# Stick-breaking attention of a two-block network in three units of key blocks, the first of them ahead of the last value slab

## What is computed

```
z = q @ k^T * 64**-0.5                            # per head, 512 x 512
log_beta = log_sigmoid(z)
log_1m = where(strict, log_sigmoid(-z), 0)        # strict: key position < query position
tail = reverse_cumsum(log_1m) - log_1m            # over the keys
a = where(strict, exp(log_beta + tail), 0)
o = a @ v;   out = concat(o over heads) @ w_out   # added to the residual
```

## Time and profile before

| what | value |
|---|---|
| time, median of 3 runs | 2701.61 us (2700.36 to 2703.32) |
| the profiled execution, its own time | 2699.93 us |
| its span in the profile | 2697.7 us |
| PE, DVE, ACT busy over the span | 97%, 58%, 34% |
| last matmul of the value slabs | 1989.12 us |
| first score of pairs 1, 4 and 5 | 2009.36, 2049.38, 2062.72 us |
| first matmul of the projection | 2106.82 us |

### The profile page before, as it was taken

One profiled execution on the slowest core, in us unless ns is written; L12 is line 12 of the kernel. 1 busy time (PEld: TensorE's weight loads), 2 busy tenths in 40 slices (PEclk: granted clock), 3 DMA queues, 4 the chain that ended last, 5 costly groups with the idle time before them and its releaser, 6 DMA issues.

```text
span 2697.7 us, 32184 instructions
## 1 busy us (share of the span) xinstructions
PE 2616.2 (97%) x12690; PEld 2142.3 (79%) x12690; DVE 1568.2 (58%) x1934; ACT 908.8 (34%) x1186; POOL 0.2 (0%) x4
## 2 busy tenths in 40 slices
PE   8999999989999999999999999999999999999999
PEld 6888887778888877877788888888876788888887
DVE  6444456676444457476564766566356566574745
ACT  4222243443222234433442423234136343432322
POOL 0000000000000000000000000000000000000000
PEclk9999999999999999999999999999999999999999
DMA  5222232003222223211331222323210132122222
GB/s 175 94 94 93 94 120 79 32 32 112 100 94 93 94 94 103 87 63 63 109 110 63 95 97 91 109 81 126 94 63 1 54 134 94 64 94 94 97 102 81
DMA packets 36595, 240.67 MB, mean 89 GB/s; under 512 B 3952, under 2 KB 6912, under 8 KB 8320
## 3 DMA queue, kind: packets, MB, share of 16 engines
q1 hardware_dynamic: 35008, 234.12, 25.3%
q10 hardware_dynamic: 1472, 4.94, 0.5%
HBM read 236.94 MB, written 2.10 MB: 89 GB/s over the span
## 4 chain that ended last, share of the span: by engine, by line
PE 89%; DVE 7%; ACT 2%; issue 1%; DMA 0%; SPq 0%; DVEq 0%; ACTq 0%
PE ps L469 24%; PE ps L471 23%; PE ps L470 23%; PE ps L1028 1%; PE ps L981 1%; PE ps L953 1%; PE ps L487 1%; PE ps L486 1%; PE ps L485 1%; PE ps L497 1%; PE ps L1013 1%; PE ps L581 1%; PE ps L583 1%; PE ps L582 1%; DVE w_lo L1663 1%
## 5 line engine op out<-in xcount | busy, mean ns | idle before, releaser
L469 PE MATMUL ps<-op_hi,w_hi 128*128 128x512 f32 x2160 | 854.0, 395 | 21.1 <-DVE op_lo L1577 15.2
L470 PE MATMUL ps<-op_lo,w_hi 128*128 128x512 f32 x2160 | 844.0, 391 | 0.0
L471 PE MATMUL ps<-op_hi,w_lo 128*128 128x512 f32 x2160 | 843.8, 391 | 0.0
L1082 ACT ACTIVATE w_hi<-w_raw 128x2048 fp32r<-128x2048 f32 x217 | 414.2, 1909 | 527.5 <-PE ps L471 394.7
L1663 DVE TENSOR_TENSOR w_lo<-w_raw,w_hi 128x2048 fp32r<-128x2048 f32 x217 | 497.0, 2292 | 32.5 <-ACT w_hi L1082 17.2
L469 PEld LDWEIGHTS ps<-op_hi,w_hi 128*128 128x128 f32 x2160 | 407.7, 189 | 113.2 <-issue 20.3
L470 PEld LDWEIGHTS ps<-op_lo,w_hi 128*128 128x128 f32 x2160 | 407.6, 189 | 89.1 <-issue 4.9
L471 PEld LDWEIGHTS ps<-op_hi,w_lo 128*128 128x128 f32 x2160 | 407.4, 189 | 85.8
L1628 DVE SCALAR_TENSOR_TENSOR x<-ps,x 128x512 f32<-128x512 f32 x134 | 92.6, 691 | 347.3 <-PE ps L471 339.5
L469 PE MATMUL ps<-h_hi,w_hi 128*128 128x512 f32 x692 | 273.4, 395 | 0.0
L471 PE MATMUL ps<-h_hi,w_lo 128*128 128x512 f32 x692 | 273.4, 395 | 0.0
(11 more groups left out here) (285 smaller groups left out, 2951.3 us busy)
## 6 DMA issues: line engine op xcount, KB each, us to landing
w_raw<-in_wstream_dram SPq DMA_DIRECT2D x217, 1024.0 KB, 4.9
w_raw<-in_wstream_dram SPq DMA_DIRECT2D x8, 256.0 KB, 7.2
x<-in_x_dram SPq DMA_DIRECT2D x4, 512.0 KB, 6.8
cr_m<-in_mem_dram ACTq DMA_DIRECT2D x2, 1024.0 KB, 4.7
out_dram<-x SPq DMA_DIRECT2D x3, 512.0 KB, 2.6
ev_s<-in_alibi_dram ACTq DMA_DIRECT2D x1, 1024.0 KB, 4.8
m_c<-in_rope_dram ACTq DMA_DIRECT2D x1, 704.0 KB, 4.0
pl_p<-in_p_dram ACTq DMA_DIRECT2D x1, 512.0 KB, 3.5
```

The costliest lines, as they stand in the source:

```text
L469: mm_(o, w_hi[:, c % 4, w], hi[:, k, 0:cols], start=(k == 0), stop=False)
L470: mm_(o, w_hi[:, c % 4, w], lo[:, k, 0:cols], start=False, stop=False)
L471: mm = mm_(o, w_lo[:, c % 4, w], hi[:, k, 0:cols], start=False, stop=(k == kt - 1))
L1082: f_(w_hi[:, c % 4, :], w_raw[:, c % 2, :], ACT.Copy).then_inc(w_hi_ready, 1)
```

## The change

Blocks 3 and 2 become one unit of 384 columns in one pair of banks; block 1 and block 0 are units of their own, with 384 and 512 columns (`UNITS`). Each unit keeps its banks: unit 0 has 4 and 5, unit 1 has 6 and 7, unit 2 has 2 and 3 (the ones of the value slab before the last). The out results take banks 0 and 1 by turns. Unit u of pair t waits for the weights of unit u of pair t - 1. ACT and DVE handle a unit with one instruction where they had two for blocks 3 and 2.

The softplus of unit 0 has places of its own for even t (`od_s_even`, `od_hi_even`, `od_lo_even`), over buffers that are free then and not over `op_hi`. The scores of units 0 and 1 of pair 0 stand ahead of the last value slab on PE, and unit 0's softplus on ACT and DVE runs beside that slab; DVE also makes `w_lo` of the second slab of three still ahead before it. The mask matrix is rounded earlier. PE's order per pair becomes

```diff
-TRI = 13 * P
-TRI_A = 11 * P
+TRI = 10 * P
+FAR = 3 * P
+UNITS = [(3, 2), (1,), (0,)]
+UNIT_COLUMNS = [FAR, 3 * P, 4 * P]
+UNIT_AT = [0, FAR, FAR + 3 * P]
...
-Z_BANKS = [4, 6, 0]
...
-def cut_at(t, kb):
-
-    return [9 * P, 6 * P, 2 * P * (1 + t % 2), P * (t % 2)][kb]
...
-def weight_at(t, kb):
-
-    return [7 * P, 4 * P, 2 * P, P * (t % 2)][kb]
+def block_at(kb):
+
+    return [2, 1, 0, 0][kb], P if kb == 2 else 0
...
+        with ExitStack() as s:
+            od_s_even = sb("od_s_even", [P, 2, FAR], FP32, s)
+        with ExitStack() as s:
+            od_lo_even = sb("od_lo_even", [P, 2, FAR], FP32R, s)
...
+        with ExitStack() as s:
+            od_hi_even = sb("od_hi_even", [P, 2, FAR], FP32R, s)
...
+        def unit_bank(u):
+
+            return [4, 6, pair_of(AT_ODD + ODD_SLABS - 2)][u]
+
+        def unit_z(u):
+
+            return ps[:, unit_bank(u):unit_bank(u) + 2, 0:UNIT_COLUMNS[u]]
+
+        def stick_bank(t):
+
+            return pair_of(AT_ODD + ODD_SLABS - 1) + t % 2
+
+        def unit_parts(t, u):
+
+            at, w = UNIT_AT[u], UNIT_COLUMNS[u]
+            if u == 0 and t % 2 == 0:
+                tiles = (od_s_even, od_hi_even, od_lo_even)
+            else:
+                tiles = (od_s, od_hi, od_lo)
+            return [tile[:, :, at:at + w] for tile in tiles]
...
-            for d in range(8, 12):
+            for d in range(8, 11):
                 to_positions(AT_ODD + d)
-            pe.wait_ge(acc_free, AT_ODD + ODD_SLABS + 2)
...
-                return Z_BANKS[(NB * t + NB - 1 - kb) % len(Z_BANKS)]
...
+            def stick_scores(t, u):
+                if t:
+                    pe.wait_ge(a_made, 3 * (t - 1) + u + 1)
+                for kb in UNITS[u]:
+                    b, at = unit_bank(u), block_at(kb)[1]
+                    for j in range(2):
+                        mm_(ps[:, b + j, at:at + SEQ - kb * P], od_k[64 * j:64 * j + 64, t, kb * P:(kb + 1) * P],
+                            od_q[64 * j:64 * j + 64, t, kb * P:SEQ], start=(kb == UNITS[u][0]), stop=False,
+                            skip_group_check=True)
...
+                mm.then_inc(z_done, 1)
...
+            def stick_exponent(t, u):
+
+                pe.wait_ge(softplus_cut, 3 * t + u + 1)
...
+                    for kb in UNITS[u]:
+                        z = block_at(kb)[1]
+                        for b in range(kb, NB):
+                            (of, at), w = block_at(b), SEQ - b * P
+                            a0 = z + (b - kb) * P
+                            _, hi, lo = unit_parts(t, of)
+                            for part in (hi, lo):
+                                mm = mm_(ps[:, unit_bank(u) + j, a0:a0 + w], od_later[:, 0 if b == kb else 1, :],
                 mm.then_inc(arg_ready, 1)
...
-                pe.wait_ge(a_made, NB * (t + 1))
+                pe.wait_ge(a_made, 3 * t + 3)
-                for kb in range(NB):
-                    at, w = weight_at(t, kb), SEQ - kb * P
+                for kb in reversed(range(NB)):
+                    (of, at), w = block_at(kb), SEQ - kb * P
+                    at += UNIT_AT[of]
                     for j in range(2):
-                        mm = mm_(ps[64 * j:64 * j + 64, 2 + t % 2, kb * P:SEQ],
+                        mm = mm_(ps[64 * j:64 * j + 64, stick_bank(t), kb * P:SEQ],
...
             pe.wait_ge(later_ready, 1)
-            for kb in (3, 2):
-                stick_scores(0, kb)
+            stick_scores(0, 0)
+            stick_scores(0, 1)
+            to_positions(AT_ODD + ODD_SLABS - 1)
+            n["op"] += KT
+            pe.wait_ge(acc_free, AT_ODD + ODD_SLABS + 1)
             for t in range(PAIRS):
-                stick_exponent(t, 3)
-                stick_scores(t, 1)
-                stick_scores(t, 0)
+                if t:
+                    stick_scores(t, 1)
+                stick_scores(t, 2)
+                if t == 1:
+                    pe.wait_ge(acc_free, AT_ODD + ODD_SLABS + 2)
                 if t:
                     stick_out(t - 1)
+                stick_exponent(t, 0)
+                if t < PAIRS - 1:
+                    stick_scores(t + 1, 0)
+                stick_exponent(t, 1)
                 stick_exponent(t, 2)
-                stick_exponent(t, 1)
-                if t < PAIRS - 1:
-                    stick_scores(t + 1, 3)
-                    stick_scores(t + 1, 2)
-                stick_exponent(t, 0)
             stick_out(PAIRS - 1)
...
-
-            act.wait_ge(aux["od_mask"], 16)
-            f_(od_later[:], od_mask[:], ACT.Copy).then_inc(later_ready, 1)
...
+                elif d == 6:
+                    act.wait_ge(aux["od_mask"], 16)
+                    f_(od_later[:], od_mask[:], ACT.Copy).then_inc(later_ready, 1)
...
-            for kb in (3, 2):
-                soft(0, kb)
...
+            soft(0, 0)
+            act.wait_ge(slab_done, AT_ODD + ODD_SLABS)
             for t in range(PAIRS):
-                weights(t, 3)
                 soft(t, 1)
-                soft(t, 0)
+                soft(t, 2)
+                weights(t, 0)
+                if t < PAIRS - 1:
+                    soft(t + 1, 0)
+                weights(t, 1)
                 weights(t, 2)
-                weights(t, 1)
-                if t < PAIRS - 1:
-                    soft(t + 1, 3)
-                    soft(t + 1, 2)
-                weights(t, 0)
...
-            for kb in (3, 2):
-                softplus(0, kb)
+            for d in range(4):
+                if d == 3:
+                    low(AT_ODD + 14)
+                    softplus(0, 0)
+                keep_rows(AT_ODD + 8 + d, od_v[:, :, d * 256:(d + 1) * 256])
+                if d < 3:
+                    low(AT_ODD + d + 11)
             for t in range(PAIRS):
                 softplus(t, 1)
-                softplus(t, 0)
+                softplus(t, 2)
                 if t:
                     stick_out(t - 1)
                 if t < PAIRS - 1:
-                    softplus(t + 1, 3)
-                    softplus(t + 1, 2)
-            stick_out(PAIRS - 1)
-            dve.wait_ge(o_read, KT)
-            for t in range(KT):
+                    softplus(t + 1, 0)
+            dve.wait_ge(arg_ready, 3 * PAIRS)
+            for t in range(KT - 1):
                 operand(t, od_q[:, t, :])
+            dve.wait_ge(stick_ready, PAIRS)
+            operand(KT - 1, ps[:, stick_bank(PAIRS - 1), :])
```

More of the change, by code:

```diff
@@ L254, in build @@
             od_later = sb("od_later", [P, 3, P], FP32R, s)
-            od_a = sb("od_a", [P, 2, TRI_A], FP32, s)
+            od_a = sb("od_a", [P, 2, TRI], FP32, s)
         ps = ctx.enter_context(nc.psum_tensor("ps", [P, 8, SEQ], FP32))
@@ L1020, in stick_exponent @@
-            def stick_exponent(t, kb):
-                w = SEQ - kb * P
-                pe.wait_ge(softplus_cut, NB * t + NB - kb)
-                for j in range(2):
-                    for b in range(kb, NB):
-                        a0, at = (b - kb) * P, cut_at(t, b)
-                        for part in (od_hi, od_lo):
-                            mm = mm_(ps[:, z_bank(t, kb) + j, a0:w], od_later[:, 0 if b == kb else 1, :],
-                                     part[:, j, at:at + w - a0], start=False, stop=True, skip_group_check=True)
+            def stick_scores(t, u):
[7 more added lines that the diff above has]
+                            skip_group_check=True)
+                    for j in range(2):
+                        mm = mm_(ps[:, b + j, at:at + P], ident_r[:], od_later[:, 2, :], start=False, stop=True,
+                                 skip_group_check=True)
+                mm.then_inc(z_done, 1)
@@ L2262, in _, with softplus @@
                 low(AT_ODD + d + 7)
[L2263 to L2273 removed]
+            def softplus(t, u):
+                buf, hi, lo = unit_parts(t, u)
+                dve.wait_ge(sp_ready, 3 * t + u + 1)
+                v.scalar_tensor_tensor(buf, buf, SOFTPLUS_LINEAR, unit_z(u), ALU.min, ALU.max).then_inc(v_step, 1)
                 done(v_step)
@@ L2276, in softplus @@
                 done(v_step)
[L2277 removed]
+                v.tensor_tensor(lo, buf, hi.bitcast(FP32), ALU.subtract).then_inc(softplus_cut, 1)
                 done(softplus_cut)
```

50 lines of the change are left out of this document (11 added, 39 removed).

## The result

| | before | changed kernel |
|---|---|---|
| time, median | 2700.35 us (2694.07 to 2705.34, 20 runs) | 2692.15 us (2689.20 to 2697.12, 20 runs) |
| ratio to before | | 0.9971, 95% interval 0.9964 to 0.9978 |
| the profiled execution | 2699.93 us, span 2697.7 | 2689.92 us, span 2688.1 |

A forecast was written before the change was run, and what follows sets the result against it. PE, busy 97% of the span, was taken as the bound. Start 6.50, pairs -0.24 and end 2.28 made 8.5 us, less 2.4 for the clock: 6.1 off, median 2695.5 us, range 2691.5 to 2701.5.

The forecast's parts named there:

- The pair: PE's period per pair: 13.38 against 13.34 us, waits of 0.84 and 0.18 gone, one of 0.97 new; six periods cost 0.24.
- 0.14 for one instruction more: On ACT and DVE: about 0.14 us of each instruction is fixed, three fall away per pair, about 0.4, hidden.
- The start: From the last value slab to pair 1: scores 1 of pair 1 at 2002.86 instead of 2009.36, 6.50 us sooner.
- The end: Last out to first projection matmul: operand 0 is cut earlier, so the projection follows the out at once, 2.28 us gained.
- The sum at full clock: Whole changed stage: 6.50 at the start, minus 0.24 in the pairs, plus 2.28 at the end, 8.5 us off.
- The clock, -2.4 at the start: Pair 0's start: one wait of 1.7 us brings PE's clock down once, costing 2.4 us of the gain.
- a period over 13.8: Pairs on PE: a sign that the forecast is wrong, pointing to clock falls or dearer handing over inside the pairs.
- rival 1: At the start: no fall of the clock, 8.5 us off, 2693.1 us; chance 0.15.
- rival 2: Pairs: clock falls in, say, two of seven, or handing over costs 0.5 more each; 3 to 4 less, 2698.9; chance 0.32.
- The rule on breaking up instructions: Unit 0's weights in each pair: two halves would be worth 0.4 us in each of seven pairs, 2.9 us.
- The range and the signs: Whole kernel: 2691.5 to 2701.5 us; chance 0.50 of faster, below 2696.2; signs include periods of 13.3 to 13.5.

The follow-up runs named there:

- e1: The changed kernel with exponent 1 ahead of the next pair's scores 0 on PE, and ACT's weights 1 moved to match; 2685.93 us, ratio 0.9948.
- e4: The changed kernel with unit 0's weights made by two ACT instructions instead of one, both waited for as before; 2691.46 us, ratio 0.9966.
- e6: The changed kernel with throw-away matmuls behind exponent 0, 7 in pair 0 and 3 in pairs 1 to 6; 2690.57 us, ratio 0.9965.
- e3: The changed kernel with the old end: last out copied to `od_q`, then all eight operands cut; 2695.10 us, ratio 0.9984.
- e9: The changed kernel with unit 0's weights made head by head, the first started once its half of exponent 0 is done; 2687.54 us, ratio 0.9955.
- e10: The edit of e9 on top of the order of e1; 2685.61 us, ratio 0.9944.
- e5: The kernel before, with throw-away matmuls in its two waits at the start of the attention; 2698.62 us, ratio 0.9992.
- e2: The changed kernel with scores of units 0 and 1 and unit 0's softplus back behind the last value slab; 2698.99 us, ratio 0.9997.
- e7: The kernel of e2 with throw-away matmuls, 7 ahead of pair 0's exponent 0 and 3 behind exponent 0 of pairs 0 to 6; 2692.34 us, ratio 0.9973.
- e8: The kernel of e1 with the late start of e2; 2688.64 us, ratio 0.9955.

## Why the prediction was right, and where it was not

- **The pair.** Right to 0.01 at full clock. Worked out: 13.38, with scores 0 at 7.42 and 0.97 of waiting against a direct start. Read: 13.37 and 13.39 by turns, 7.43. e1 took the wait away and got 12.41. Hidden where it said so: ACT and DVE save instructions, and the time shows nothing of it. Its estimate of 0.14 for one instruction more was too large for ACT (0.06 in e4); it came from DVE's lengths.
- **The start.** Right: 6.50 worked out at full clock and 6.50 read. From the last value matmul, unit 0's weights came at 3.91 (worked out 4.00), scores 0 at 4.75 (4.86), pair 1 at 10.69 (10.82). The 0.13 went to the slab, whose last matmul comes 3.05 later behind the one before it than it did (14.57 against 11.52), not 2.92.
- **The end.** Right: 2.28 both.
- **The sum at full clock**, 8.5, is what e6 shows against the trace of before: 129.22 - 120.74 = 8.48.
- **The clock, -2.4 at the start.** This step failed. It said that a wait of the same size at the same place would bring the clock down once. The changed kernel waits 1.68 there, and the clock stayed up, as it did at this place in the five other traces with the early start that have nothing filled in (e1, e3, e4, e9, e10); what came in its trace was 3.4 us in pair 6, at 1.57. That is one of the signs that the prediction had named for being wrong: a period over 13.8. So rival 1 was right of the start (its 2693.1 is nearest to the median), and rival 2 right in kind of the pairs, with one fall and not two. The row taken for the price was at fault too: 2.4 was added up from three groups that ran slowly, but 0.97 of it only shortened a wait for DVE behind them. e5 measures 1.45. A loss on PE counts to the next wait that another engine ends, and the prediction's own rows of waits (three exponents waiting for `od_lo`) showed one right there.
- **What it counted as nothing.** The start's 6.50 was added up from waits and matmuls at full clock, and nothing in it says that the early start itself changes the clock. Without it the same kernel loses 6.8 us, of which about 5 is clock (e2, e7), part of it in later pairs. At the end it counted the wait of 2.2 and not the fall that can follow it, 1.5 us in the traces of e3 and e5. At full clock on both sides the change is worth 127.77 - 120.74 = 7.0 us, and the other 1.45 of the 8.5 is the fall at the start that it removed.
- **The rule on breaking up instructions** (the Trainium skill, Perfetto Trace Analysis, Optimizing Scalar/DVE Operations). The prediction gave it 0.4 for each of seven pairs. e9 shows 0.32 in each of six full periods, 1.9 in all, when the first piece also starts sooner; e4 shows that a cut alone costs 0.06. So the rule, which says only that breaking up may help, agrees with these runs. But reordering (e1) was worth 0.97 at the same place, and with it the cut is worth nothing (e10).
- **The range and the signs.** 2692.15 lies in 2691.5 to 2701.5, near its lower end; faster by over 0.2%, as half the chance had it. That the total came near is in part luck: the fall at the start that it took off did not come, and one in pair 6 did. Of the 3.4 us between 2695.5 and 2692.15, 1.3 is the median of before that it started from.

## What to carry to other kernels

When a merge or a change of buffers puts a wait between a group and the next one that needs its banks, look for a group whose operands are ready and put it in between before cutting instructions up: that one exchange (e1, two lines moved) brought another 6.2 us, three quarters of what the whole change had brought. Price a slow stretch from its start to the next wait that another engine ends, not by adding up the slow rows. And where idle time stands at the edge between two stages, test what it does to the clock by filling it with matmuls that nobody reads: it costs one run, moves nothing, and tells waits from clock.

## What the runs showed of the hardware

- With 2.9 us of scores, and the softplus of unit 0, ahead of the last slab, TensorE's clock stayed at 2.4 GHz at the start in all six traces with nothing filled in (changed, e1, e3, e4, e9, e10); with them behind it, it fell to 1.2 GHz for 10.2 us in e2 and e8, and for 6.8 in before. Filling the idle time kept it up too, in e5 and e7.
- The length of a single wait doesn't foretell it. Waits of 1.68 (changed), 1.74 (e4, e9) and 2.08 (e5) at the start passed without a fall, one of 1.71 (e2, e8) was followed by one. The wait of 2.21 ahead of the projection was followed by one in e3 and e5, and not in before. The sequence of a pair is the same six times, with a wait of 0.90; in the traces of the changed kernel and e3 pair 6 alone fell, in e2 pairs 1 and 6, and in e4, with waits of 0.96, none. What decides between such equal rows stays open.
- A fall costs what the rows behind it can't absorb: 1.57 for 3.4 us in a pair, where no other wait follows before the period ends; 3.1 for 6.8 us in pair 6 of e2; 1.45 for 6.8 us at the start of before; 4.1 for 10.2 us in e2 and 3.7 in e8.
- Two ACT instructions on the same banks, one behind the other without a wait, took 0.87 where one took 0.81.
- Ahead of the stage the falls change from one execution to the next: 34 to 48 us at the lower clock, and 1965.4 to 1969.7 us from the first matmul to the stage, in twelve traces with the same work on PE up to that point. The 8 us spread of the changed kernel's executions goes with the clock: 2689.20 to 2690.90 where the mean granted clock was 0.993, 2692.04 to 2697.12 where it was 0.990. Where in those executions the falls lay is not on record.
